# Eight more columns ahead of the split rows: a shift of 32 bytes in on-chip memory

## What is computed

```
p       = h @ w_in                     # block 1: [256, 1024] x [1024, 5632]
y_a     = fourier_mix(u_f) @ w_fourier
y_b     = (b_g * centred_conv3(c_g * v, w_conv)) @ w_conv_out
x       = x + gate_m * ((gate_a * y_a + gate_b * y_b) @ w_o)
moe     = per expert: (silu(xe @ w_gate_e) * (xe @ w_up_e)) @ w_down_e      # 32 tokens each
# block 2
proj    = rms_norm_2(x, norm_pre) @ w_in_2
m       = sigmoid(gate_a) * (y_a @ w_a) + sigmoid(gate_b) * (y_b @ w_b);  x = x + rms_norm_2(m @ w_o, ...)
# block 3, two layers
qkv..   = h @ w_in_3 ;  x = x + mix @ w_o_3
x       = x + (silu(h @ w_gate_3) * (h @ w_up_3)) @ w_down_3               # 2816 wide
```

## The kernel before

| rows | used in | moving or stationary | bytes beyond the ring within 512, before |
|---|---|---|---|
| `xR` in `cols3` | block 1, 2, 3; gate and up of the feed-forward part | moving | 192 |
| `xR` in `rows3` | block 1, 2, 3 | stationary | 192 |
| `fmR` (Fourier rows) | block 1, `wf` | moving | 256 |
| `convH`, `convL` | block 1, `wc` | moving | 192, 256 |
| `yR` | block 2, `wa`, `wb` | moving | 192 |
| `mixR` | block 3, `wo3` | stationary | 192 |
| `actR` | block 3, down projection | stationary | 0 |

## Time and profile before

### The profile page before, as it was taken

How to read it: one execution, slowest core, us unless ns; L and a number is a source line. 1 busy time by engine, 2 the same in 40 slices (tenths; PEclk the granted TensorE clock), 3 DMA queues, 4 the chain that set the end, 5 groups by cost and what they waited for, 6 DMA issues and landing times.

```text
span 2117.7 us, 32656 instructions
## 1 busy us (share of the span) xinstructions
PE 1699.7 (80%) x13430; PEld 1226.0 (58%) x13430; DVE 808.9 (38%) x1592; ACT 646.7 (31%) x1144; POOL 83.9 (4%) x143
## 2 busy tenths in 40 slices
PE   6999876566565666656666799988999999999998
PEld 4889822111111211111111599988989988989996
DVE  3364621001110111100111457775666654666664
ACT  3334410000000000000000347655654434655433
POOL 2000010000000000000000200101100001000000
PEclk9999987877878787787777899999999999989999
DMA  9987789999999999999999953408065545145640
GB/s 362 349 320 247 286 367 427 429 429 428 429 428 430 427 429 427 429 428 428 428 428 429 324 199 120 140 19 285 21 199 183 192 155 191 41 149 180 198 180 21
DMA packets 154178, 613.49 MB, mean 290 GB/s; under 512 B 8848, under 2 KB 64346, under 8 KB 129496
## 3 DMA queue, kind: packets, MB, share of 16 engines
q1 hardware_dynamic: 150112, 604.47, 72.5%
q0 software_dynamic: 3200, 7.14, 1.1%
q10 hardware_dynamic: 760, 0.39, 0.1%
HBM read 610.88 MB, written 5.03 MB: 291 GB/s over the span
## 4 chain that ended last, share of the span: by engine, by line
PE 54%; DMA 38%; DVE 3%; ACT 2%; issue 1%; DVEq 1%; POOL 0%; SPq 0%; POOLq 0%; ACTq 0%
PE psum L1483 52%; DMA ring<-in_w_up_e 19%; DMA ring<-in_w_down_e 19%; DMA ring<-in_w_ada 1%; PE psum L1855 1%; DVE ring_r L707 1%; ACT arena L1080 0%; ACT ring_r L698 0%; PE psum L1588 0%; POOL stat L954 0%; DVE arena L2461 0%; SPq L777 0%; PE psum L2019 0%; PE psum L2004 0%; DVE xR_r L2078 0%
## 5 line engine op out<-in xcount | busy, mean ns | idle before, releaser
L1483 PE MATMUL psum<-ring,arena 128*32 128x512 f32 (+2 forms) x4314 | 542.1, 647 | 275.2 <-DMA ring<-in_w_up_e 122.8
L1483 PE MATMUL psum<-xR_r,ring_r 128*128 128x256 f32 x4416 | 539.7, 281 | 2.0 <-DVE xR_r L2099 1.2
L1483 PEld LDWEIGHTS psum<-xR_r,ring_r 128*128 128x128 f32 x4416 | 517.9, 189 | 12.8 <-issue 10.8
L1483 PEld LDWEIGHTS psum<-ring,arena 128*32 128x32 f32 x4314 | 154.9, 134 | 629.9 <-issue 210.9
L707 DVE TENSOR_TENSOR ring_r<-ring,ring_r 128x1024 fp32r<-128x1024 f32 (+2 forms) x332 | 378.0, 1172 | 188.0 <-ACT ring_r L698 187.3
L698 ACT CAST ring_r<-ring 128x1024 fp32r<-128x1024 f32 (+2 forms) x332 | 320.4, 1008 | 376.6 <-PE psum L1483 370.1
L1483 PE MATMUL psum<-arena 128*128 128x256 f32 (+7 forms) x1270 | 188.7, 375 | 20.2 <-DVE arena L2336 9.9
L2333 DVE TENSOR_TENSOR arena<-arena,psum 128x512 f32<-128x512 f32 x16 | 16.9, 1054 | 482.2 <-PE psum L1483 482.2
L1483 PE MATMUL psum<-ring_r,xR_r 128*128 128x256 f32 (+3 forms) x1344 | 172.8, 284 | 8.5 <-DVE xR_r L2084 5.0
L1483 PE MATMUL psum<-ring_r,arena_r 128*128 128x512 f32 (+1 forms) x912 | 168.1, 345 | 2.1 <-DVE mt L2712 2.1
L1483 PEld LDWEIGHTS psum<-ring_r,xR_r 128*128 128x128 f32 x1344 | 162.5, 190 | 11.3 <-DVE ring_r L707 5.1
(11 more groups left out here) (270 smaller groups left out, 953.9 us busy)
## 6 DMA issues: line engine op xcount, KB each, us to landing
ring<-in_w_gate_e SPq DMA_DIRECT2D x64, 2048.0 KB, 25.8
ring<-in_w_down_e SPq DMA_DIRECT2D x63, 2048.0 KB, 26.3
ring<-in_w_up_e SPq DMA_DIRECT2D x62, 2048.0 KB, 24.9
ring<-in_w_in SPq DMA_DIRECT2D x29, 2048.0 KB, 12.4
ring<-in_w_ada SPq DMA_DIRECT2D x12, 2048.0 KB, 14.1
ring<-in_w_gate SPq DMA_DIRECT2D x22, 1024.0 KB, 5.4
ring<-in_w_up SPq DMA_DIRECT2D x22, 1024.0 KB, 8.1
ring<-in_w_down SPq DMA_DIRECT2D x10, 2048.0 KB, 7.8
```

The lines of the kernel that those rows point to most:

```text
L1483: return nc.tensor.matmul(o, l, r, start=s, stop=e)
```

## The change

The tensor `stat` gets 488 columns instead of 480. That moves `xR`, `mt2` and `arena` by 32 bytes, so that each begins 224 bytes beyond the ring's place within 512. `act_at`, the column at which `actR` begins in the arena, goes down by 8, so `actR` and all that lies behind it in block 3 keep their addresses. No instruction is added, taken away or moved on any engine: every engine has the same instructions in the same order, and only addresses differ.

```diff
-        stat = sb("stat", 480)
+        stat = sb("stat", 488)
         x_moe, xR = twice("xR", 2 * KT * T)
...
         mixR = R(3 * D, KT)
-        act_at = 3 * D + 80
+        act_at = 3 * D + 72
         actR = R(act_at, FT)
...
-            assert _p[0] <= 480
+            assert _p[0] <= 488
```

## The result

| | before | after |
|---|---|---|
| median, runs | 2122.62 us, 8 | 2135.21 us, 8 |
| lowest to highest | 2117.17 to 2130.27 | 2133.08 to 2139.52 |
| ratio to before | | 1.0055, interval 1.004 to 1.007 |
| profiled execution, span | 2119.53, 2117.7 | 2133.08, 2131.3 |

The change makes the kernel 12.6 us slower. The three runs of before that stood ahead of the prediction had a median 5 us above that of all eight.

The account below looks back on a forecast made before the run. The prediction took DMA to bound the experts and TensorE the dense stretches. Its terms summed to 26.0 us, 23.5 after a tenth off; with 4.2 us more on the profiled 2119.5 it forecast 2147 us, range 2116 to 2165.

Parts of the forecast that it names:

- What bounds the kernel: Whole kernel: DMA bounds the experts (300 to 1190 us), TensorE the dense stretches at 100 to 231 and 1597 to 1712 us.
- the level at 224 bytes: Matmuls with `xR` streamed: taken as 119.9 ns, the level at 256, with bounds of 113.5 and 126 ns.
- gate and up, 2016: Gate and up, twice 1008 matmuls: from 113.5 to 119.9 ns each, +12.9 us.
- the other 2400 with `xR` streamed: Remaining matmuls streaming `xR`: from a mean of 116.0 ns, 3.9 ns more each, +9.4 us.
- arena rows streamed, 480: Matmuls streaming `arena_r`: 0 for `wf`, 0.4 us for `wc`, 1.0 us for `wa` and `wb`.
- rows loaded, 1536: Matmuls with ring streamed and rows loaded: from 118.4 to 119.9 ns as offset goes 320 to 288, +2.3 us.
- What was taken off: Whole sum: a tenth off for pieces ending in a wait and the start near DMA, 26.0 to 23.5 us.
- middle: All runs with rows moving lock at 118.4 ns: 16.6 us, nine tenths 15, giving 2135 to 2143 us; chance 0.12.
- Nothing: Levels depend on how a run starts, not on offsets, so the mix stays: 2128 us; chance 0.20.
- Faster: At 224 and 288 bytes all matmuls run at 113.5 ns: 14 us less, 2114 or 2106 us; chance 0.18.
- A start off 64 bytes: Such a start costs by itself, 126 ns in all 6432 matmuls: 58 us, up to 2186 us; chance 0.08.
- The absolute time: Whole kernel: profiled 2119.5 us plus 23.5 plus 4.2, half the 8.3 us to the median, giving 2147 us.

Follow-up runs that it names:

- the map: Eight kernels, each the before kernel with `xR` at 0, 64, 128, 160, 176, 208, 256 or 320 bytes beyond the ring: ratios 1.0022 to 1.0121.
- the kernel at 256: Before kernel with `stat` at 496 columns, so rows lie 256 bytes beyond the ring: 2149.37 us, ratio 1.0121.
- the last kernel: Before kernel with `xR` left at 192 bytes, Fourier and low convolution rows moved from 256 to 192, `mixR` from 192 to 320: 2120.58 us, ratio 0.9989.

## Why the prediction was wrong in its size

**What bounds the kernel** held. TensorE's distances in dense runs carried the change; VectorE's 512-column operations and the landing of the first expert's units, put at zero, stayed at zero (VectorE is busy 808.6 us beside 808.9).

**The step that failed is the level at 224 bytes.** I took 119.9 ns, the level at 256, on the ground that a place 32 bytes from a bad one should be like it. In gate and up it measured 118.4 ns in both layers. The same was done for the arrays that go to 288 bytes, and there it missed by more, even by the sign. The neighbours could not have given the number: 16 bytes beside 192 are slower than 32 bytes beside it (119.3 at 208, 118.4 at 224), and 160 is better than 176. (This rests on the two kernels whose rows begin off 32 bytes; the map in steps of 32 bytes alone would allow a curve between its places.) The rows of before could not have told 118.4 from 119.9; the range between 113.5 and 126 was the honest thing and the value taken in it only a guess.

Term by term:

| term | forecast | measured |
|---|---|---|
| gate and up, 2016 | +12.9 | +10.0 |
| the other 2400 with `xR` streamed | +9.4 | 15.8 - 10.0 = +5.8 |
| arena rows streamed, 480 | +1.4 | +0.8 |
| rows loaded, 1536 | +2.3 | -0.5 |
| sum | 26.0 | 16.1 |
| on the path | 23.5 | 13.6 in the profile, 12.6 in the medians |

The level at 224 accounts for 6.5 us of the 9.9 between the sums: 1.5 ns too much for each of 4416 matmuls. The rows loaded have a sign of their own: they went from 320 to 288 bytes and from 118.4 to 117.3 ns, and the Fourier rows also were faster at 288 than at 256 (116.7 against 119.9 ns). "Nearer to 256, so slower" was the same guess. For the convolution rows the forecast of 119.9 came close to the 120.0 measured, but by luck, since neither of their two distances has that level.

**What was taken off** for the path was of the right size, but not shown to be right. The span grew by 13.6 us where the matmuls were busy for 16.1 more, 15% less instead of a tenth, and the profile has the difference in two places. The experts, from their first matmul with weights to the first matmul behind them, took 916.45 us before (274.86 to 1191.31) and 914.58 after (277.24 to 1191.82). The stretch from the first down projection to the second gate and up took 220.68 us before and 218.78 after. Neither need come from the change: the experts took 913.1 to 916.4 us in the other kernels' profiles, in no order of their distances. Nor do they hide a delay of block 1 as a rule: in the kernel at 256 they began 5.8 us later than before (280.62) and ended 5.5 us later (1196.79).

**The rivals.** The rival that came out is the *middle* one, which had a chance of 0.12: it said one level of 118.4 ns, and 2135 to 2143 us. The measured 118.4 ns and 2135.21 us are its numbers. Part of that is luck: its 118.4 was the upper level at 192, read from pieces of 48, and the upper level of a long run at 192 turned out to be 117.9, so 224 has a level of its own. *Nothing* falls with the map: the same code at 0 or 256 bytes has no dense run at the lower level. Its own observation, that there are two levels at one distance, is true and stands beside the mechanism instead of against it; that the start of a run picks the level was not shown. The rule that it leaned on is in the Trainium skill ("TensorE: Matmul & The Clock Gate", step-by-step section: two independent read ports). The prediction drew from it that addresses can't matter, and that does not fit these rows: the same 1008 matmuls take 114.5 to 121.2 us by address alone. The 109.2 ns of the prediction come from that page's formula for a matmul by itself; for loads and matmuls in pairs, as here, the page says that both set the distance, so that figure was no forecast for them. *Faster* falls, with its idea that the slow places are multiples of 128 and all others good. *A start off 64 bytes* falls with the kernel in which everything moved.

**The absolute time.** I put half of the 8.3 us between profile and median on top, for a gate and up at the upper level in the timed runs. The median of eight runs of before is only 3.1 us above the profiled execution, and that of the changed kernel 2.1, so of the 12.0 us between 2147.2 and 2135.2 the path has 9.9 and this term 2.1. The reading of it fits: at 192 bytes the eight runs of before spread over 13 us (2117.17 to 2130.27), at 0 bytes four runs over 4 us (2145.89 to 2149.74), and one layer's level is worth 4.5 us. That the levels make this spread was not shown, since one execution of each kernel was traced.

**Still open.** What picks the level when a run starts at an odd multiple of 64 bytes was not found. In block 1, where a short float32 product stands between the pieces, they took the upper and the lower level in strict turn before, and in the opposite turn in the last kernel. A way to pick the lower level each time would be worth at most about 2400 x 2.5 ns + 1536 x 4 ns, some 12 us, an estimate from the rows of before, and no experiment here tried one. Why the convolution rows, which change between two distances, were slower at 224 and 288 than runs at either of these was not found. Which part of memory or engine makes the two streams meet is not shown either, only that their distance does it.

## What to carry to other kernels

Where float32r matmuls of 256 columns follow each other without a pause and each has its own weight load, look at the distance between matmuls, not at their duration, and set the streamed and the loaded array an odd multiple of 64 bytes apart within 512 (64 and 192 reached the lower level here with the rows streamed, 192, 320 and 448 with the rows loaded). Measure the layout: the cost of a place was not to be had from its neighbours here, and 16 bytes took the gain away. When a table ahead of such arrays grows, pad it so that the distance stays.

## What the runs showed of the hardware

- The distance from one 256-column float32r matmul to the next was 113.4 to 120.1 ns at a granted clock of 1.00, by nothing but the offset between the streamed and the loaded operand: 120.1 ns at 0 and 256 bytes, 118.8 at 128, 113.4 or 117.9 at 64 and 192, 117.9 at 320 (113.9 there with the rows loaded), and 117.4 to 119.4 at 160, 176, 208 and 224.
- A run whose matmuls change between two offsets need not take the mean of their levels: at 224 and 288 bytes the convolution rows took 120.0 ns, where runs at one of them took 118.4 and 116.7.
- Moving both operands together by 32 bytes changed nothing: 114.53 us for the 1008 in both kernels.
- With 512 columns streamed and the operands at one offset, 264 matmuls took 60.1 us before and after, (60.12 - 0.39) / 263 = 227 ns (0.39 us is one such matmul's own time), twice the best distance of 256 columns.
- A dense run kept its level for over 100 us, and the same code in one execution can take one level in the first layer and the other in the second.
